# Second block's attention: decay added to masks on GpSimd, division before the turn, values stationary on column halves

## The chip, the cores and the metric

One NeuronCore of a Trainium2 chip runs the kernel. The metric is the device time of one execution in microseconds, median of several; less is better. The engines are TensorE (PE; its weight loads are listed as PEld), VectorE (DVE), ScalarE (ACT), GpSimd (POOL) and SyncE (SP), which only issues DMAs here. Each works through its own queue in program order and waits on semaphores.

## What is computed

Two blocks of two layers each, one sequence of 256 tokens, 1024 features, all in float32. The change lies in the hybrid mixer of the second block. It has four heads of causal attention with rotary positions (A), four heads of forgetting attention (B), a gated branch (C) and a pooling branch (D); the parts that matter, shortened:

```python
def forgetting_attention(q, k, v, log_f):          # 4 heads of 64, 256 tokens
    c = jnp.cumsum(log_f, axis=-1)
    ...
        logits = (jnp.einsum('bhqd,bhkd->bhqk', qc, k) * scale
                  + cq[..., :, None] - c[..., None, :])
        logits = jnp.where(kpos[None, :] <= qpos[:, None], logits, -jnp.inf)
        p = jax.nn.softmax(logits, axis=-1)
        return jnp.einsum('bhqk,bhkd->bhqd', p, v)

def hybrid_mixer(x, w_in, ...):
    z = x @ w_in
    aq, ak, av, bq, bk, bv, bf, cu, cv, dp = jnp.split(z, IN_SPLITS, axis=-1)
    ya = moba_attention(rotary(aq), rotary(ak), av)     # causal softmax attention here
    yb = forgetting_attention(bq, bk, bv, log_sigmoid(bf + b_forget))
    yc = causal_spatial_gating(gelu(cu), gelu(cv), ...)
    yd = multiscale_pool(dp, pool_w, pool_scale)
    return jnp.concatenate([ya, yb, yc, yd], axis=-1) @ w_o
```

The softmax of a row doesn't change when a number is added to all of it, so of the decay only `-c[k]`, one row of 256 numbers for each head, has to be added to the scores.

## The kernel before

All weights stream through in **units** of 128 x 1024 numbers. SyncE loads a unit into `w_raw` (4 buffers), ScalarE rounds it to `w_hi` (`hi_next`), VectorE makes the difference `w_lo` (`lo_next`, line 1114), and TensorE multiplies with both, so that a float32 product is three float32r ones. `w_hi` and `w_lo` have 6 buffers. ScalarE rounds unit `u` when TensorE has finished unit `u-6`, so ScalarE's and VectorE's steps run beside TensorE's units, and weights are ready about five units ahead.

A second-block mixer (`mixer2`, one for each of two layers) has 26 units. Each engine's program is one loop over unit numbers `i`, with the attention's steps written in at fixed numbers. On TensorE, units 4 to 13 give q and k of four head pairs and the pooling input, 14 to 17 the values `v_tok`, 18 to 25 the output projection over the branches in the order C, D, A, B (`K_OUT`). The steps between, ahead of the unit of that number:

- units 8, 10, 12, 14: `scores(pair)`. Two heads of a pair lie on the two halves of the partitions and run together. For the forgetting pairs 2 and 3 a second product adds the decay: `head_sel` (a column of ones and zeros) times `neg_rows`, the rounded rows of `-c`, which VectorE writes in `split_decay`.
- units 10 to 17: `turn_a(h)`, three transposes of head `h`'s probabilities `sm`. It waits on the exp (`e2_ready`).
- unit 19: `values()`: for each head the turned probabilities `aT8` are the weights and 64 columns of `v_tok` move; the result has tokens on partitions.
- unit 21: `turn_o()`: eight transposes of `o_tok` bring the result to features on partitions.

On VectorE, step `i` holds `attn_mask(i-8)` (adds the causal mask to the scores, takes the row maximum and its negative) for steps 8 to 15, then the weight difference, then what else is due: the rotary steps at 7 and 9 (ahead of the weight difference), `sgu_scale` at 11, the window sums of branch D at 14 and 15, `c_rest` at 15, `o_scale` at 19 (division by the row sums and a factor, token by token), `o_rest` at 21. On ScalarE, step `i` holds a weight rounding, then `attn_store(i-10)`, then `attn_exp(i-8)`, which also sums the rows into `den`. GpSimd clears pads and masks one weight at the start of the mixer and has nothing to do after that, but for a parameter load later on.

## Time and profile before

| | us |
|---|---|
| median of 3 runs | 1910.05 (1909.76 to 1910.22) |
| profiled execution: its span, first to last instruction | 1908.1 |
| TensorE busy | 1899.0 |
| VectorE busy | 1312.4 |
| ScalarE busy | 1112.2 |
| GpSimd busy | 8.6 |

The profile gives its own execution's time as the span; the timed runs' median stands 1.95 us above it. The page counts an instruction busy from start to end, and matmuls overlap: a start of one to a start of the next is what an instruction costs the queue. Times in the rows are from the span's start. A float32 product stands in the trace as two matmuls (two passes) and a transpose as one. The form `128*64` behind a matmul is the part of the array used, rows by columns.

### The profile page before, as it was taken

What the parts mean: (1) busy time and instruction counts of PE and PEld (TensorE: products, weight loads), DVE (VectorE), ACT (ScalarE), POOL (GpSimd) and SP (SyncE); (2) the same over time, 40 slices, a digit from 0 to 9 for tenths busy, and PEclk for the clock granted to TensorE, in tenths of its full rate; (3) what the DMA queues carried; (4) which work ended last, traced back from release to release, by engine and by line L of the source; (5) the groups of instructions that cost most, each with busy time, mean ns of one, the idle gap of its engine ahead of it and who ended that gap; (6) DMA issues with size and microseconds to landing.
All of it is one profiled execution on the core that took longest, in us unless ns stands there. A gap on an engine that the chain in (4) does not pass through costs nothing.

```text
span 1908.1 us, 26525 instructions
## 1 busy us (share of the span) xinstructions
PE 1899.0 (100%) x10072; PEld 1610.6 (84%) x10072; DVE 1312.4 (69%) x2238; ACT 1112.2 (58%) x1738; POOL 8.6 (0%) x22
## 2 busy tenths in 40 slices
PE   9999999999999999999999999999999999999998
PEld 7888899888888888888988888888988888988887
DVE  6555887585755575558876767555868888868887
ACT  6444766554644564457764556445747666747664
POOL 0000000000000000000000000000000000000000
PEclk9999999999999999999999999999999999999999
DMA  8555445545655555555455446554535555535552
GB/s 303 190 188 183 161 140 168 166 154 188 206 188 187 177 188 188 187 166 177 133 177 164 159 163 218 199 190 153 177 111 190 193 190 194 179 111 189 192 193 100
DMA packets 92654, 337.74 MB, mean 177 GB/s; under 512 B 10288, under 2 KB 10544, under 8 KB 92400
## 3 DMA queue, kind: packets, MB, share of 16 engines
q1 hardware_dynamic: 91152, 329.49, 52.0%
q0 software_dynamic: 1232, 6.47, 1.0%
q8 instruction: 81, 1.33, 0.3%
q14 instruction: 45, 0.37, 0.1%
q10 hardware_dynamic: 144, 0.09, 0.0%
HBM read 334.96 MB, written 1.05 MB: 176 GB/s over the span
## 4 chain that ended last, share of the span: by engine, by line
PE 98%; DVE 1%; ACT 0%; DMA 0%; issue 0%; DVEq 0%; SPq 0%; ACTq 0%
PE stream L1971 14%; PE stream L1973 14%; PE stream L1972 14%; PE acc L1971 9%; PE acc L1973 9%; PE acc L1972 9%; PE stream L2457 7%; PE stream L2458 4%; PE stream L1965 4%; PE stream L1966 3%; PE stream L1967 3%; PE stream L2063 1%; PE acc L2175 1%; PE stream L1991 1%; PE acc L2224 0%; PE acc L2457 0%
## 5 line engine op out<-in xcount | busy, mean ns | idle before, releaser
L1114 DVE TENSOR_TENSOR w_lo<-w_raw,w_hi 128x1024 fp32r<-128x1024 f32 x623 | 759.0, 1223 | 371.1 <-ACT w_hi L585 369.1
L585 ACT ACTIVATE w_hi<-w_raw 128x1024 fp32r<-128x1024 f32 x623 | 654.7, 1055 | 389.4 <-PE stream L1973 271.7
L1971 PE MATMUL stream<-w_hi,h_both 128*128 128x512 f32 x1024 | 405.0, 396 | 0.0
L1973 PE MATMUL stream<-w_lo,h_both 128*128 128x512 f32 x1024 | 399.0, 390 | 0.0
L1972 PE MATMUL stream<-w_hi,h_both 128*128 128x512 f32 x1024 | 398.8, 389 | 0.0
L1971 PEld LDWEIGHTS stream<-w_hi,h_both 128*128 128x128 f32 x1024 | 192.3, 188 | 41.6 <-DVE h_both L1597 0.8
L1973 PEld LDWEIGHTS stream<-w_lo,h_both 128*128 128x128 f32 x1024 | 192.2, 188 | 40.8
L1972 PEld LDWEIGHTS stream<-w_hi,h_both 128*128 128x128 f32 x1024 | 192.5, 188 | 37.8
L2457 PE MATMUL stream<-h_both,w_hi 128*128 128x512 f32 x608 | 216.1, 398 | 0.0
L1971 PE MATMUL acc<-w_hi,act_hi 128*128 128x512 f32 x528 | 211.1, 400 | 0.3
L1973 PE MATMUL acc<-w_lo,act_hi 128*128 128x512 f32 x528 | 206.3, 391 | 0.0
L1972 PE MATMUL acc<-w_hi,act_lo 128*128 128x512 f32 x528 | 206.2, 390 | 0.0
L2458 PE MATMUL stream<-h_both,w_lo 128*128 128x256 f32 x608 | 170.6, 281 | 0.0
L1965 PE MATMUL stream<-h_both,w_hi 128*128 128x256 f32 x544 | 159.1, 292 | 0.0
L1966 PE MATMUL stream<-h_both,w_hi 128*128 128x256 f32 x544 | 153.7, 283 | 0.0
L1967 PE MATMUL stream<-h_both,w_lo 128*128 128x256 f32 x544 | 153.7, 283 | 0.0
L2457 PEld LDWEIGHTS stream<-h_both,w_hi 128*128 128x128 f32 x608 | 114.2, 188 | 27.6
L1971 PEld LDWEIGHTS acc<-w_hi,act_hi 128*128 128x128 f32 x528 | 99.2, 188 | 21.8 <-DVE w_lo L1114 1.9
L1973 PEld LDWEIGHTS acc<-w_lo,act_hi 128*128 128x128 f32 x528 | 99.1, 188 | 21.7
L2458 PEld LDWEIGHTS stream<-h_both,w_lo 128*128 128x128 f32 x608 | 114.8, 189 | 1.4
L1972 PEld LDWEIGHTS acc<-w_hi,act_lo 128*128 128x128 f32 x528 | 99.3, 188 | 17.9
L1965 PEld LDWEIGHTS stream<-h_both,w_hi 128*128 128x128 f32 x544 | 104.0, 191 | 2.0 <-issue 1.2
(347 smaller groups left out, 2433.7 us busy)
## 6 DMA issues: line engine op xcount, KB each, us to landing
w_raw<-in_w_up SPq DMA_DIRECT2D x264, 512.0 KB, 3.4
w_raw<-in_w_mix SPq DMA_DIRECT2D x228, 512.0 KB, 3.4
w_raw<-in_w_down SPq DMA_DIRECT2D x132, 512.0 KB, 3.4
params<-in_params POOLq DMA_DIRECT2D x4, 859.5 KB, 6.1
x_residual<-in_x SPq DMA_DIRECT2D x4, 256.0 KB, 5.5
constants<-in_params POOLq DMA_DIRECT2D x2, 512.0 KB, 8.7
last_gain_bias<-in_last POOLq DMA_DIRECT2D x1, 1024.0 KB, 5.1
out_x<-y_tok SPq DMA_DIRECT2D x4, 256.0 KB, 2.1
```

Of the source, the lines that this page charges most:

```text
L585: nc.scalar.activation(w_hi[:, u % RING], w_raw[:, u % RAW], ACT.Copy).then_inc(hi_ready, 1)
L1114: nc.vector.tensor_tensor(w_lo[:, u % RING], w_raw[:, u % RAW], w_hi[:, u % RING].bitcast(F32), ALU.subtract).then_inc(split_done, 1)
L1965: nc.tensor.matmul(dst, w_hi[:, s, w], hi, start=first, stop=False)
L1966: nc.tensor.matmul(dst, w_hi[:, s, w], lo, start=False, stop=False)
L1967: return nc.tensor.matmul(dst, w_lo[:, s, w], hi, start=False, stop=last)
L1971: nc.tensor.matmul(dst, hi, w_hi[:, s, w], start=first, stop=False)
L1972: nc.tensor.matmul(dst, lo, w_hi[:, s, w], start=False, stop=False)
L1973: return nc.tensor.matmul(dst, hi, w_lo[:, s, w], start=False, stop=last)
L1991: r = nc.tensor.transpose(turned[q][:, half(j)], y_tok[:, t, (4 * q + j) * P:(4 * q + j + 1) * P], ident)
L2063: r = nc.tensor.transpose(dst, cbuf[:, 2 * (c % 2) + t, half(i)], ident)
L2457: nc.tensor.matmul(dst, w_hi[:, u % RING, w], h_both[:, k], start=(k == 0), stop=False)
L2458: r = nc.tensor.matmul(dst[:, 0:T], w_lo[:, u % RING, w], h_hi[:, k], start=False, stop=(k == KT - 1))
```

## The change

- The decay is no longer multiplied onto the scores. GpSimd stores the four rows of `-c` to DRAM, loads them back to all 128 partitions (`mask_keys`), and adds the causal mask to them; `attn_mask` of heads 4 to 7 uses these instead of `mask_rows`. The rounded rows, the selector and `split_decay` are gone.
- The probabilities are divided by their row sums before they are turned: VectorE takes the reciprocal of a head's two columns (`invert`, at the start of step 9+h), GpSimd multiplies `sm` in place, and `turn_a` waits for GpSimd (`p_divided`) in place of the exp.
- In `values()` the 64 columns of `v_tok` are the weights and the turned probabilities move, 256 and 128 columns; the two heads of a pair write to the two halves of the partitions. The result already has features on partitions. `turn_o`, `o_tok` and `o_scale` are gone; ScalarE and VectorE round the result from PSUM with the factor `BRANCH`, at step 20 instead of 21.

```diff
...
@@ -479,7 +478,7 @@
 
         V_FM, V_C1, V_OUT = 4, 14, 18
         FM_UNITS = 10
-        HEAD_AT, TURN_AT, VALUES_AT, OUT_TURN_AT = 8, 10, 19, 21
+        HEAD_AT, TURN_AT, VALUES_AT, OUT_AT = 8, 10, 19, 20
         K_OUT = (4, 5, 6, 7, 0, 1, 2, 3)
         EVICTIONS = 2 + FM_UNITS + 2
 
...
@@ -1003,10 +1002,10 @@
                                                  scale=pool_sc[:, ct:ct + 1])
                     r.then_inc(cd_hi, 1)
 
-                def o_round(t):
-                    act.wait_ge(o2_turned, l * 2 + t + 1)
-                    nc.scalar.activation(ya_hi[:, 0:4, half(t)], bank[2 * t + 1][:].rearrange("p (k q) -> p k q", k=4),
-                                         ACT.Copy).then_inc(o2_hi, 1)
+                def o_round(g):
+                    act.wait_ge(o2_ready, l * 2 + g + 1)
+                    nc.scalar.activation(ya_hi[:, 2 * g:2 * g + 2].rearrange("p a t -> p (a t)"), bank[2 * g][:],
+                                         ACT.Copy, scale=BRANCH).then_inc(o2_hi, 1)
 
                 def take_gelu(t):
                     if t == 0:
...
@@ -1699,17 +1698,6 @@
                     dve.wait_ge(f_vec, l * 3 + 2)
                     nc.vector.tensor_scalar(neg_c[:], row2_c[:], -1.0 / A_SCALE, None, ALU.mult).then_inc(f_vec, 1)
 
-                def split_decay():
-                    dve.wait_ge(f_vec, l * 3 + 3)
-                    if l == 0:
-                        dve.wait_ge(neg_cleared, 1)
-                    for b in (0, 64):
-                        nc.vector.tensor_copy(neg_rows[b:b + 4], neg_c[:]).then_inc(neg_split, 1)
-                    dve.wait_ge(neg_split, l * 4 + 2)
-                    for b in (32, 96):
-                        nc.vector.tensor_tensor(neg_rows[b:b + 4], neg_c[:], neg_rows[0:4].bitcast(F32),
-                                                ALU.subtract).then_inc(neg_split, 1)
-
                 def groups(ap):
                     return ap.rearrange("p a (g c) -> p a g c", c=64)
 
...
@@ -1777,10 +1765,13 @@
                     dve.wait_ge(s2_ready, l * 8 + h + 1)
                     if h >= 2:
                         dve.wait_ge(a2_turned, l * 8 + h - 1)
+                    if h == 4:
+                        dve.wait_ge(decay_ready, (l + 1) * 2)
+                    mask = mask_rows if h < 4 else mask_keys[:, h - 4]
                     nc.vector.memset(spare[:, 13 + b:14 + b], 0.0)
                     for qt, (lo, hi) in enumerate(((0, P), (P, 3 * P))):
                         r = nc.vector.tensor_tensor_reduce(
-                            out=sm[:, b, lo:hi], in0=side[b][:, lo:hi], in1=mask_rows[:, lo:hi], scale=1.0,
+                            out=sm[:, b, lo:hi], in0=side[b][:, lo:hi], in1=mask[:, lo:hi], scale=1.0,
                             scalar=-3e38, op0=ALU.add, op1=ALU.max,
                             accum_out=mx[:, 2 * b + qt:2 * b + qt + 1])
                     r.then_inc(s2_masked, 1)
...
@@ -1818,30 +1809,20 @@
                                                            op0=ALU.mult, op1=ALU.subtract)
                     r.then_inc(cd_split, 1)
 
-                def o_scale():
-                    dve.wait_ge(e2_ready, l * 8 + 8)
-                    nc.vector.reciprocal(rden[:], den[:]).then_inc(dve_step, 1)
-                    dve.wait_ge(dve_step, stepped())
-                    nc.vector.tensor_scalar(rden[:], rden[:], BRANCH, None, ALU.mult).then_inc(dve_step, 1)
-                    dve.wait_ge(dve_step, stepped())
-                    for t in range(QT):
-                        dve.wait_ge(o2_ready, l * 2 + t + 1)
-                        nc.vector.tensor_tensor(o_tok[:, t].rearrange("p (h d) -> p h d", h=HEADS),
-                                                bank[2 - 2 * t][:].rearrange("p (h d) -> p h d", h=HEADS),
-                                                rden[:, :, t].unsqueeze(2).to_broadcast([P, HEADS, 64]),
-                                                ALU.mult).then_inc(o2_scaled, 1)
-
-                def o_rest(t):
-                    dve.wait_ge(o2_hi, l * 2 + t + 1)
-                    nc.vector.tensor_tensor(ya_lo[:, 0:4, half(t)], bank[2 * t + 1][:].rearrange("p (k q) -> p k q", k=4),
-                                            ya_hi[:, 0:4, half(t)].bitcast(F32), ALU.subtract).then_inc(ab_split, 1)
-
-                if l == 0:
-                    for b in (0, 64):
-                        r = nc.vector.tensor_tensor(head_sel[b:b + 64], ident[b:b + 64, b:b + 4],
-                                                    ident[b:b + 64, b + 32:b + 36], ALU.add)
-                    r.then_inc(sel_ready, 1)
+                def invert(h):
+                    dve.wait_ge(e2_ready, l * 8 + h + 1)
+                    nc.vector.reciprocal(rden[:, h], den[:, h]).then_inc(den_ready, 1)
+
+                def o_rest(g):
+                    dve.wait_ge(o2_hi, l * 2 + g + 1)
+                    nc.vector.scalar_tensor_tensor(out=ya_lo[:, 2 * g:2 * g + 2].rearrange("p a t -> p (a t)"),
+                                                   in0=bank[2 * g][:], scalar=BRANCH,
+                                                   in1=ya_hi[:, 2 * g:2 * g + 2].rearrange("p a t -> p (a t)").bitcast(F32),
+                                                   op0=ALU.mult, op1=ALU.subtract).then_inc(ab_split, 1)
+
                 for i in range(U_MIX2 - LAG + 1):
+                    if HEAD_AT < i <= HEAD_AT + HEADS:
+                        invert(i - HEAD_AT - 1)
                     if HEAD_AT <= i < HEAD_AT + HEADS:
                         attn_mask(i - HEAD_AT)
                     if i == 7:
...
@@ -1919,6 +1896,22 @@
                 w = p2("sgu_w", 0, 4 * P).rearrange("p (g t) -> p g t", g=4)
                 nc.gpsimd.tensor_tensor(w, w, mask_cols.unsqueeze(1).to_broadcast([P, 4, P]),
                                         ALU.mult).then_inc(sgu_w_masked, 1)
+                pool.wait_ge(f_vec, l * 3 + 3)
+                pool.dma_start(decay_dram[l], neg_c[:]).then_inc(decay_out, 16)
+                pool.wait_ge(decay_out, (l + 1) * 16)
+                pool.dma_start(mask_keys[:, :, 0:P], decay_dram[l][:, 0:P].partition_broadcast(P)).then_inc(decay_in, 16)
+                pool.dma_start(mask_keys[:, :, P:], decay_dram[l].partition_broadcast(P)).then_inc(decay_in, 16)
+                pool.wait_ge(decay_in, (l + 1) * 32)
+                for c in (slice(0, P), slice(P, 3 * P)):
+                    nc.gpsimd.tensor_tensor(mask_keys[:, :, c], mask_keys[:, :, c],
+                                            mask_rows[:, c].unsqueeze(1).to_broadcast([P, 4, c.stop - c.start]),
+                                            ALU.add).then_inc(decay_ready, 1)
+                for h in range(HEADS):
+                    b = h % 2
+                    pool.wait_ge(den_ready, l * 8 + h + 1)
+                    for t, c in enumerate((slice(0, P), slice(P, 3 * P))):
+                        r = nc.gpsimd.tensor_scalar(sm[:, b, c], sm[:, b, c], rden[:, h, t:t + 1], None, ALU.mult)
+                    r.then_inc(p_divided, 1)
 
             pool.wait_ge(raw_full[2], 3 * 16)
             pool.dma_start(cst[:, 3 * P:C_LATE], consts[:, 3 * P:C_LATE]).then_inc(consts_in, 16)
...
@@ -2539,36 +2530,24 @@
                     r.then_inc(swapped, 1)
 
                 def scores(pair):
-                    forgets = pair >= 2
                     q, k = 2 * pair, 2 * pair + 1
                     if pair == 0:
                         pe.wait_ge(f_vec, l * 3 + 2)
                     else:
                         pe.wait_ge(s2_masked, l * 8 + 2 * pair)
-                    if forgets:
+                    if pair >= 2:
                         pe.wait_ge(m2_evict, e0 + 2 + k + 1)
-                        pe.wait_ge(neg_split, l * 4 + 4)
-                        pe.wait_ge(sel_ready, 1)
                     else:
                         pe.wait_ge(rot_done, l * 2 + pair + 1)
                     for qs, ks, c in ((slice(P, T), T, slice(P, 3 * P)), (slice(0, P), P, slice(0, P))):
                         for j in range(2):
                             r = slice(64 * j, 64 * j + 64)
-                            i = nc.tensor.matmul(side[j][:, c], qk[r, q, qs], qk[r, k, 0:ks], start=True,
-                                                 stop=not forgets)
-                            if ks == P and not forgets:
+                            i = nc.tensor.matmul(side[j][:, c], qk[r, q, qs], qk[r, k, 0:ks], start=True, stop=True)
+                            if ks == P:
                                 i.then_inc(s2_ready, 1)
-                        if forgets:
-                            for j in range(2):
-                                r = slice(64 * j, 64 * j + 64)
-                                col = 2 * (pair - 2) + j
-                                i = nc.tensor.matmul(side[j][:, c], head_sel[r, col:col + 1].to_broadcast([64, P]),
-                                                     neg_rows[r, 0:ks], start=False, stop=True)
-                                if ks == P:
-                                    i.then_inc(s2_ready, 1)
 
                 def turn_a(h):
-                    pe.wait_ge(e2_ready, l * 8 + h + 1)
+                    pe.wait_ge(p_divided, l * 8 + h + 1)
                     if h > 0:
                         pe.wait_ge(a2_stored, l * 8 + h)
                     for b in range(3):
...
@@ -2579,22 +2558,15 @@
                     pe.wait_ge(m2_evict, e0 + EVICTIONS)
                     pe.wait_ge(a2_stored, l * 8 + HEADS)
                     pe.wait_ge(cd_split, l * 2 + 2)
-                    for h in range(HEADS):
-                        c = slice(64 * h, 64 * h + 64)
-                        r = nc.tensor.matmul(bank[2][:, c], aT8[:, h, 0:P], v_tok[:, 0, c], start=True, stop=True)
-                    r.then_inc(o2_ready, 1)
-                    for h in range(HEADS):
-                        c = slice(64 * h, 64 * h + 64)
-                        nc.tensor.matmul(bank[0][:, c], aT8[:, h, P:T], v_tok[:, 0, c], start=True, stop=False)
-                        r = nc.tensor.matmul(bank[0][:, c], aT8[:, h, T:], v_tok[:, 1, c], start=False, stop=True)
-                    r.then_inc(o2_ready, 1)
-
-                def turn_o():
-                    for t in range(QT):
-                        pe.wait_ge(o2_scaled, l * 2 + t + 1)
-                        for k in range(4):
-                            r = nc.tensor.transpose(bank[2 * t + 1][:, blk(k)], o_tok[:, t, blk(k)], ident)
-                        r.then_inc(o2_turned, 1)
+                    for j in range(HEADS // 2):
+                        at = j % 2 * T
+                        for keys, rows, c in ((0, slice(0, T), slice(at, at + T)), (1, slice(T, 3 * P), slice(at + P, at + T))):
+                            for h in (2 * j, 2 * j + 1):
+                                z = 64 * (h % 2)
+                                r = nc.tensor.matmul(bank[j // 2 * 2][z:z + 64, c], v_tok[:, keys, 64 * h:64 * h + 64],
+                                                     aT8[:, h, rows], start=keys == 0, stop=keys == 1)
+                        if j % 2:
+                            r.then_inc(o2_ready, 1)
 
                 def mixed(u):
                     k = K_OUT[u - u0 - V_OUT]
@@ -2603,7 +2575,7 @@
                 def arrived(u):
                     k = K_OUT[u - u0 - V_OUT]
                     if k < 4:
-                        pe.wait_ge(ab_split, l * 2 + 2)
+                        pe.wait_ge(ab_split, l * 2 + k // 2 + 1)
                     else:
                         pe.wait_ge(cd_split, l * 2 + (k - 4) // 2 + 1)
 
@@ -2635,8 +2607,6 @@
                         pooling()
                     if i == VALUES_AT:
                         values()
-                    if i == OUT_TURN_AT:
-                        turn_o()
                     u = u0 + i
                     unit(u)
                     if i < V_C1:
```

Left out are the declarations: `decay_dram` (a DRAM tensor for each layer) and `mask_decayed` come, `o_tok`, `neg_rows`, `head_sel` and their semaphores go, and `OUT_TURN_AT`, 21, becomes `OUT_AT`, 20.

VectorE's queue at the end of the heads, steps 15 and 16 of a mixer, before (`w_lo` is a weight difference, `pool_sums` and `pooled` the window sums, `ya_lo` the rest of branch C):

```order
L1788 TENSOR_SCALAR neg_max<-row_max 128x2
L1114 TENSOR_TENSOR w_lo<-w_raw,w_hi 128x1024
L1798 SCALAR_TENSOR_TENSOR pool_sums<-constants,pool_in 128x256
L1803 TENSOR_TENSOR pooled<-pool_sums 64x256 x2
L1809 TENSOR_TENSOR pooled<-pooled,constants 128x512
L1811 TENSOR_TENSOR pooled<-pooled,pool_in 128x512
L1755 SCALAR_TENSOR_TENSOR ya_lo<-acc,ya_hi 128x512
L1114 TENSOR_TENSOR w_lo<-w_raw,w_hi 128x1024 x2
```

and in the changed kernel, from the same instruction on, the mask of head 7:

```order
L1779 TENSOR_SCALAR neg_max<-row_max 128x2
L1113 TENSOR_TENSOR w_lo<-w_raw,w_hi 128x1024
L1789 SCALAR_TENSOR_TENSOR pool_sums<-constants,pool_in 128x256
L1794 TENSOR_TENSOR pooled<-pool_sums 64x256 x2
L1800 TENSOR_TENSOR pooled<-pooled,constants 128x512
L1802 TENSOR_TENSOR pooled<-pooled,pool_in 128x512
L1743 SCALAR_TENSOR_TENSOR ya_lo<-acc,ya_hi 128x512
L1814 RECIPROCAL row_scales<-row_sums 128x2
L1113 TENSOR_TENSOR w_lo<-w_raw,w_hi 128x1024 x2
```

The reciprocal of head 7 stands behind all of step 15, ahead of two weight differences.

GpSimd's queue in the first mixer, before (the last row loads the next layer's parameters):

```order
L1941 MEMSET neg_c_rounded 128x256
L1918 MEMSET pool_sums 128x2x16
L1920 ISA
L1920 TENSOR_TENSOR params<-params,constants 128x512
L1929 DMA params<-in_params 128x1719
```

and in the changed kernel (`neg_c_rows` is in DRAM; the last two rows are the division of head 0 and come eight times, once for each head):

```order
L1895 MEMSET pool_sums 128x2x16
L1897 ISA
L1897 TENSOR_TENSOR params<-params,constants 128x512
L1900 DMA neg_c_rows<-row_neg_c 4x256
L1902 DMA mask_decayed<-neg_c_rows 128x4x128
L1903 DMA mask_decayed<-neg_c_rows 128x4x256
L1906 TENSOR_TENSOR mask_decayed<-mask_decayed,constants 128x4x128
L1906 TENSOR_TENSOR mask_decayed<-mask_decayed,constants 128x4x256
L1913 TENSOR_SCALAR scores<-scores,row_scales 128x128
L1913 TENSOR_SCALAR scores<-scores,row_scales 128x256
```

Head 0's division stands behind the store, the two loads and the two sums.

## Rows read from the trace of the kernel before

**Rows 1.** The page: busy time and share by engine; the chain by engine.
```profile
PE 1899.0 (100%) x10072; PEld 1610.6 (84%) x10072; DVE 1312.4 (69%) x2238; ACT 1112.2 (58%) x1738; POOL 8.6 (0%) x22
...
PE 98%; DVE 1%; ACT 0%; DMA 0%; issue 0%; DVEq 0%; SPq 0%; ACTq 0%
```

**Rows 2.** Stretches: length, busy PE, PEld, DVE, ACT, POOL, clock, DMA share, GB/s.
```profile
1343.64:1412.51 68.87, 68.80 (x491) 63.16 (x488) 51.78 (x115) 40.92 (x84) 0.00 (x0) 1.00 0.49 161
1629.97:1698.85 68.88, 68.81 (x491) 63.17 (x488) 49.86 (x113) 39.55 (x83) 0.00 (x0) 1.00 0.46 153
```

**Rows 3.** Timeline, PE: start, length, line, result<-operands; scores and turns.
```profile
1364.00 0.92 PE L2557 MATMUL acc<-qk 64*128 64x256 f32 x8
1364.85 0.55 PE L2575 MATMUL stream<-constants,scores 128*128 128x128 f32 x3
...
1371.39 0.70 PE L2557 MATMUL acc<-qk 64*128 64x256 f32 x4
...
1372.43 0.55 PE L2575 MATMUL stream<-constants,scores 128*128 128x128 f32 x3
```

**Rows 4.** Timeline, PE: values, the next unit, and the turn of the result.
```profile
1398.25 1.89 PE L2584 MATMUL stream<-v_tok,attn_T 128*128 128x64 f32 x16
...
1403.52 0.48 PE L1971 MATMUL acc<-w_hi,ya_hi 128*128 128x512 f32 x1
...
1409.10 1.04 PE L2596 MATMUL stream<-constants,o_tok 128*128 128x128 f32 x8
...
1410.20 0.39 PE L1972 MATMUL acc<-w_hi,ya_lo 128*128 128x512 f32 x1
```

**Rows 5.** Timeline, PE: first block's gate rows; full-width 256-column passes (L2537).
```profile
224.65 1.95 PE L2151 MATMUL stream<-x_residual,params 128*64 128x256 f32 x16
...
226.75 0.28 PE L1966 MATMUL stream<-h_both,w_hi 128*128 128x256 f32 x1
...
1352.38 1.03 PE L2537 MATMUL acc<-qk,constants 128*128 128x256 f32 x4
...
1353.36 0.28 PE L1966 MATMUL stream<-h_both,w_hi 128*128 128x256 f32 x1
```

**Rows 6.** Timeline, DVE: weight differences behind branch C; a reciprocal.
```profile
1390.86 2.40 DVE L1114 TENSOR_TENSOR w_lo<-w_raw,w_hi 128x1024 fp32r<-128x1024 f32 x2
...
1400.73 0.25 DVE L1823 RECIPROCAL row_scales<-row_sums 128x16 f32<-128x16 f32 x1
```

**Rows 7.** Timeline, PE: the turn of head 7.
```profile
1390.68 0.49 PE L2575 MATMUL stream<-constants,scores 128*128 128x128 f32 x3
```

**Rows 8.** Timeline, POOL: its work at the start of the first mixer.
```profile
1330.32 0.31 POOL L1941 MEMSET neg_c_rounded<- 128x256 f32 x1 [118.26 <-PE acc L1973]
...
1330.74 1.08 POOL L1920 TENSOR_TENSOR params<-params,constants 128x512 f32<-128x512 f32 x1
```

**Rows 9.** Timeline, DVE, beside GpSimd's sum and after it.
```profile
1330.75 0.35 DVE L1152 SCALAR_TENSOR_TENSOR x_residual<-stream,gains,x_residual 128x128 f32<-128x128 f32 x1
1331.01 0.90 DVE L1118 TENSOR_SCALAR h_both<-x_residual,gains 128x128 fp32r<-128x128 f32 x1
...
1332.35 0.28 DVE L1118 TENSOR_SCALAR h_both<-x_residual,gains 128x128 fp32r<-128x128 f32 x1
```

**Rows 10.** Timeline, DVE: the decay rows; two steps of pair 1's rotation.
```profile
1351.85 0.28 DVE L1700 TENSOR_SCALAR row_neg_c<-row_c 4x256 f32<-4x256 f32 x1
...
1362.44 0.69 DVE L1771 TENSOR_TENSOR qk<-qk,constants 128x512 f32<-128x512 f32 x1
1363.16 0.69 DVE L1773 TENSOR_TENSOR qk<-qk,rotated 128x512 f32<-128x512 f32 x1
```

**Rows 11.** DMA issues: what, queue, count, size, us from issue to landing.
```profile
constants<-in_params POOLq DMA_DIRECT2D x2, 512.0 KB, 8.7
last_gain_bias<-in_last POOLq DMA_DIRECT2D x1, 1024.0 KB, 5.1
out_x<-y_tok SPq DMA_DIRECT2D x4, 256.0 KB, 2.1
```

25 lines of the change are left out of this document (9 added, 16 removed).

## The prediction

> **What bounds the kernel now.** I read the page first: TensorE is busy for the whole span and holds 98% of the chain that ended last [rows 1]. Then the busy times of the two stretches that the change touches, unit 4 to unit 22 of each second-block mixer: TensorE 68.80 of 68.87 us and 68.81 of 68.88 us, at a granted clock of 1.00, which is the 2.4 GHz level [rows 2]. So there is no wait on TensorE to win. What the change takes off TensorE's queue comes off the time, and every wait that it adds there is paid in full. VectorE (52 us) and ScalarE (41 us) have room on average, but not everywhere, and GpSimd does nothing in these stretches. Last I read the timeline around the places that change. Both mixers show the same rows, 286 us apart on TensorE, so each term is worked out for the first and taken twice.
>
> **What leaves TensorE.** (a) The decay products. Scores of pair 1, which has none, go from 1364.00 to the next instruction at 1364.85, 0.85 us; pair 2, with them, from 1371.39 to 1372.43, 1.04 us [rows 3]. Two pairs: 0.38 us.
> (b) The values. They now run from 1398.25 to 1403.52, 5.27 us: 24 products of 64 columns, each split into two passes, so that 0.11 us a pass is mostly the change of weights [rows 4]. The new form exists already in the first block: the gate rows, 8 products with 64 stationary columns written to partition halves, 256 moving columns, 16 passes. They take from 224.65 to 226.63 (0.12 before the matmul at 226.75), 1.98 us, where a full-width pass of 256 columns takes 0.215 (four from 1352.38 to 1353.24) and 16 of them would take 3.44 [rows 5]. So two halves do run side by side, and 1.98 holds the way in and out. The new values have as many such passes, 1.98, and 16 of 128 columns; eight 128-column passes in a row take 0.87 [rows 4], which two at a time prices 16 at. Together 2.85, so 2.42 us less.
> (c) The turn of the result: from 1409.10 to 1409.97 (0.23 before 1410.20), 0.87 us [rows 4].
> A mixer saves 0.38 + 2.42 + 0.87 = 3.67 us on TensorE, two save 7.3. VectorE also loses the rounding of the decay rows, the scaling of the result and its reciprocal, and gains eight small reciprocals; weights and rounding run units ahead, so of these only the ones inside the head chain below count.
>
> **What is added: a divide between exp and turn.** Before, a head's chain was mask (VectorE), exp (ScalarE), turn (TensorE). Now it is mask, exp, reciprocal (VectorE), two multiplications (GpSimd), turn. The turn of head h waits on TensorE, ahead of unit 10+h, and all units queue behind it. I went through the heads by asking when VectorE gets to the reciprocal, since it stands in program order at the start of step 9+h. Heads 1 to 6 have most of two units between exp and turn, more than the new steps need. Head 7 has nothing left: its reciprocal stands behind the whole of the window sums and the rest of branch c. VectorE ends those at 1390.86, where it now goes on to two weight differences [rows 6], while TensorE starts turn 7 at 1390.68 [rows 7]. In the changed kernel VectorE has one more reciprocal (head 6) ahead of that, 0.2, and the one of head 7, 0.2 (a reciprocal of 128x16 took 0.25 [rows 6]): 1391.25. GpSimd's two multiplications have 384 columns. By the clearing of 256 columns in 0.31 they take 0.46, by the sum of two operands over 512 in 1.08 they take 0.81 [rows 8]; one operand and a result lie between, I take 0.65. That gives 1391.9 against 1390.68 - 0.38 = 1390.3 for TensorE: **a wait of 1.6 us** if nothing else is in the way.
> Something is. While GpSimd's sum ran (1330.74 to 1331.82), a VectorE multiplication that reads and writes SBUF alone took 0.90 instead of 0.28 and ended with it; a VectorE instruction with one operand from PSUM took its usual 0.35 beside the same sum [rows 8, 9]. So the two engines hold each other up on SBUF. Right behind the reciprocal of head 7 VectorE goes into two weight differences, all in SBUF, 2.40 us [rows 6]. They are ready and start at once; GpSimd needs a semaphore first. If they hold up GpSimd as its sum held up VectorE, it gets in behind the second, or one multiplication behind each: 1391.25 + 2.4 + 0.65 = 1394.3, **a wait of 4.0 us**. The ends are 1.6 and 4.0; I take 4.0, since the row nearest to a difference of two SBUF tiles is the multiplication in SBUF that was held, not the one fed from PSUM.
> The Trainium skill, SBUF — State Buffer, section "Who interferes with whom", goes further than the row: a VectorE instruction with two SBUF inputs and a GpSimd instruction that reads SBUF exclude each other for a whole instruction, and the one that started first goes on. By it the wait is the 4.0 of the sum above; if it held for VectorE's two-port modes alone, which is all that the row shows, it would be the 1.6.
>
> **What is added: decay rows through DRAM.** GpSimd's queue holds, in this order, the store of the rows, a wait for it, two broadcast loads, a wait for them, two sums, then the divide of head 0. So head 0, which needs no decay at all, and TensorE's turn 0 behind it, wait for the whole transfer. The rows are ready at 1352.13 [rows 10]. The store: a small store took 2.1 (256 KB) [rows 11], 1354.2. The loads, 0.79 MB in 1024 pieces: issue 0.6, and 5.1 to landing as for 1 MB, 8.7 at worst [rows 11]; I take 5.1 as the nearest in size: 1359.9. The sums: 512 and 1024 columns at 1.08 per 512, 3.2 us: 1363.1. The divide 0.65: 1363.8, against turn 0 at 1364.85 [rows 3]. **Wait 0**; with 8.7 it would be 2.5.
> The Trainium skill, DMA: Bandwidth & Descriptors, "Anatomy of one DMA — SWDGE (gpsimd) path", prices a GpSimd DMA at 2.0 us plus its bytes over 436 GB/s, 3.8 us for the loads; the divide would then end at 1362.5, and the wait stays 0.
> The sums have a second price. They fall on 1359.9 to 1363.1, where VectorE rotates pair 1 (1362.44, 1363.16, both in SBUF [rows 10]) and TensorE's scores of pair 1 start at 1364.00, 0.15 us behind the rotation's end. The reciprocal of head 0 stands ahead of it as well, 0.2. So TensorE waits between 0.2 (no hindrance) and 2.4 (a rotation step that finds the longer sum just begun, 2.2 more). I take the middle, **1.3 us**, because the sums cover the first of the two steps for half of their length.
> The mask of head 4 needs the sums only behind turn 2, at 1372.43 [rows 3], and between the values and the reader of the newly rounded result stand three units, of which 19 and 20 alone take 1403.52 to 1409.10 [rows 4], more than two evictions on ScalarE and VectorE need: both at no price, the first at one for one if the sums came after 1372.43.
>
> **The sum.** Per mixer -3.67 + 4.0 + 1.3 + 0 = +1.6, twice +3.3 us. Made against the span of 1908.1 us that is 1911.4, and the time stands 1.95 us above the span, as the median of the runs does now: 1913.4 us. Some 0.2% (3.8 us) is what a measurement of this kernel can tell from no change, so the forecast lies at the edge of it.
>
> **Rivals.**
> 1. No mutual hindrance with weight differences and rotations: waits of 1.6 and 0.2, -3.67 + 1.8 = -1.9 per mixer, 1906.3 us, faster. For it: the VectorE instruction with PSUM input was not slowed. Against: the one in SBUF was, threefold.
> 2. The loads land late (1024 small pieces where the rows have 128 large ones, beside weight traffic). It decides from a landing about 1 us after 1359.9. At 8.7 the divide ends at 1367.4; the rotation is then free of the sums (0.2), turn 0 waits 2.3 to 3.5, per mixer +2.9 to +4.0: 1916 to 1918 us, slower.
> 3. TensorE's clock falls during the 4 us wait. No row shows a price, since TensorE never stands still here. If the lower level, 1.2 GHz, lasted as long as the wait, 2 us per mixer are lost: 1917 us.
> 4. The halves don't run side by side: values 16 x 0.215 + 16 x 0.11 = 5.2, nothing saved in (b), 1918 us. [rows 5] speak against it.
>
> **How the numbers follow.** Forecast 0.50 (its own range 1910.5 to 1917: the rotation term alone gives 2 us either way), rival 1 0.27, rival 2 0.13, rival 3 0.07, rival 4 0.03. Of the forecast's share about half lies over 1913.9 (slower), of rival 1's a little over half under 1906.2 (faster), and rivals 2 to 4 are nearly all slower: slower 0.25 + 0.21 = 0.46, faster 0.16, same 0.38. The range takes in rival 1 with a shorter GpSimd price and rivals 2 to 4 at their middle: 1905.5 to 1919.
>
> **What would show it.** TensorE's idle time ahead of turn 7: 4 us (forecast) or 1.6 (rival 1), its releaser GpSimd's second multiplication. GpSimd's multiplications of head 7 starting only after a weight difference ends, or weight differences longer than 1.2 us beside them. Idle time ahead of scores 1 released by a rotation that is longer than 0.69 us [rows 10]. Values 2.85 us. The first sum starting at about 1360; after 1361, rival 2. What would make it wrong most easily is the size of the hindrance, which rests on one row.

## The result and the profile after

| | us |
|---|---|
| changed kernel, median of 4 runs | 1926.55 (1924.31 to 1928.18) |
| the kernel before beside it, median of 4 | 1909.91 (1909.76 to 1910.22) |
| ratio, with its 95% interval | 1.0085 [1.0073, 1.0098] |
| profiled execution of the changed kernel: span | 1922.5 (its time 1924.31) |

The change makes the kernel slower by 0.85%, about 17 us. The forecast was 1913.4, the range ended at 1919.0. The profiled execution is the shortest of the four; its span grew by 14.4 us, from 1908.1 to 1922.5, and the rest of this section says where they lie. The other three, 1.0 to 3.9 us longer, have no trace. The page, busy time and chain, against [rows 1]:

```profile
PE 1899.1 (99%) x10008; PEld 1605.9 (84%) x10008; DVE 1312.3 (68%) x2236; ACT 1113.1 (58%) x1738; POOL 55.1 (3%) x63
...
PE 92%; DVE 4%; POOL 1%; DMA 1%; ACT 1%; issue 1%; POOLq 0%; DVEq 0%; ACTq 0%
```

TensorE has 64 matmuls fewer and is busy for as long as before: either nothing was saved, or what remains runs slower. It has lost 6% of the chain to others. The saving is real. The values in the second mixer, timeline of TensorE:

```profile
1702.42 2.82 PE L2566 MATMUL stream<-attn_T,v_tok 128*64 128x256 f32 x32
1705.17 0.50 PE L1962 MATMUL acc<-w_hi,ya_hi 128*128 128x512 f32 x1
```

From 1702.42 to 1705.17 are 2.75 us where [rows 4] had 5.27. With the turn of the result (0.8) and the decay products (0.38) a mixer saves 3.7 us, as predicted; two save 7.4. The waits are in the same timeline; the last bracket is TensorE's idle time ahead of the row and who ended it. First mixer, then the second:

```profile
1365.49 0.92 PE L2545 MATMUL acc<-qk 64*128 64x256 f32 x8 [1.10 <-DVE qk L1761]
1370.08 0.90 PE L2554 MATMUL stream<-constants,scores 128*128 128x128 f32 x3 [3.66 <-POOL scores L1913]
1395.83 0.55 PE L2554 MATMUL stream<-constants,scores 128*128 128x128 f32 x3 [0.46 <-POOL scores L1913]
1402.39 0.55 PE L2554 MATMUL stream<-constants,scores 128*128 128x128 f32 x3 [3.26 <-POOL scores L1913]
...
1662.35 1.58 PE L2545 MATMUL acc<-qk 64*128 64x256 f32 x8 [1.98 <-DVE qk L1761]
1664.10 0.90 PE L2554 MATMUL stream<-constants,scores 128*128 128x128 f32 x3 [0.17 <-POOL scores L1913]
1688.14 0.55 PE L2554 MATMUL stream<-constants,scores 128*128 128x128 f32 x3 [0.46 <-POOL scores L1913]
1694.70 0.55 PE L2554 MATMUL stream<-constants,scores 128*128 128x128 f32 x3 [3.26 <-POOL scores L1913]
```

In order: scores of pair 1, then turns 0, 6 and 7. Before there was no such bracket here. They add up to 14.35 us. Rows 1370.08 and 1664.10 show something else: three transposes take 0.90 us where they took 0.55. The stretches behind the waits tell why (length, busy time of PE, PEld, DVE, ACT, POOL, then the granted clock, DMA share and GB/s):

```profile
1370.08:1374.90 4.82, 4.82 (x23) 4.82 (x24) 2.08 (x8) 1.48 (x5) 2.93 (x4) 0.50 0.37 136
1374.90:1376.00 1.10, 1.10 (x8) 1.10 (x8) 0.00 (x0) 0.00 (x0) 0.00 (x0) 0.62 0.73 291
...
1402.39:1403.40 1.01, 1.01 (x6) 0.90 (x7) 0.00 (x0) 0.42 (x1) 0.00 (x0) 0.83 0.74 199
1403.40:1405.60 2.20, 2.20 (x7) 1.72 (x6) 0.27 (x1) 0.91 (x3) 0.00 (x0) 0.50 0.46 182
1405.60:1408.00 2.40, 2.40 (x10) 1.88 (x9) 0.60 (x2) 0.60 (x1) 0.00 (x0) 0.82 0.00 0
1662.30:1663.00 0.70, 0.65 (x4) 0.66 (x6) 0.70 (x1) 0.00 (x0) 0.70 (x1) 0.61 0.00 0
1663.00:1664.90 1.90, 1.73 (x12) 1.41 (x9) 0.41 (x2) 0.00 (x0) 1.90 (x3) 0.50 0.26 95
1664.90:1667.00 2.10, 2.10 (x16) 2.10 (x16) 1.82 (x7) 1.42 (x5) 0.63 (x1) 0.77 0.43 164
```

A clock of 0.50 is the 1.2 GHz level; [rows 2] had 1.00 all through. Busy time times the missing share of the clock gives what is lost: 2.83 us behind turn 0 and 1.70 behind turn 7 of the first mixer, 1.60 behind scores of pair 1 of the second, 6.1 in all. Behind turn 7 of the second mixer the clock stayed at 1.00. So -7.4 + 14.35 + 6.1 = +13.1 of the 14.4. Of the other 1.3, about 0.5 had arisen by 306 us, in the first block, which is the same in both kernels; what makes the rest is not shown.

Two timelines hold the causes. GpSimd in the first mixer (store, two loads, two sums, divisions of heads 0 and 1 together, then heads 5 and 7):

```profile
1352.35 0.58 POOL L1900 DMA_DIRECT2D neg_c_rows<-row_neg_c  x1 [20.11 <-DVE row_neg_c L1699]
1357.01 0.80 POOL L1902 DMA_DIRECT2D mask_decayed<-neg_c_rows  x1 [4.08 <-DMA neg_c_rows<-row_neg_c]
1357.81 0.77 POOL L1903 DMA_DIRECT2D mask_decayed<-neg_c_rows  x1
1363.52 4.04 POOL L1906 TENSOR_TENSOR mask_decayed<-mask_decayed,constants 128x512 f32<-128x512 f32 x2 [4.94 <-DMA mask_decayed<-neg_c_rows]
1367.54 3.97 POOL L1913 TENSOR_SCALAR scores<-scores,row_scales 128x128 f32<-128x128 f32 x4
...
1387.37 1.51 POOL L1913 TENSOR_SCALAR scores<-scores,row_scales 128x128 f32<-128x128 f32 x2 [2.48 <-DVE row_scales L1814]
...
1398.98 3.36 POOL L1913 TENSOR_SCALAR scores<-scores,row_scales 128x128 f32<-128x128 f32 x2 [3.20 <-DVE row_scales L1814]
```

and VectorE (last rotation step of pair 1, a weight difference; then the reciprocal of head 7 and the difference behind it):

```profile
1363.69 1.66 DVE L1761 TENSOR_TENSOR qk<-qk,rotated 128x512 f32<-128x512 f32 x1
1365.27 3.37 DVE L1113 TENSOR_TENSOR w_lo<-w_raw,w_hi 128x1024 fp32r<-128x1024 f32 x1
...
1398.73 0.15 DVE L1814 RECIPROCAL row_scales<-row_sums 128x2 f32<-128x2 f32 x1
1398.80 1.20 DVE L1113 TENSOR_TENSOR w_lo<-w_raw,w_hi 128x1024 fp32r<-128x1024 f32 x1
```

A head's two multiplications take 1.51 us when nothing disturbs them, and 3.36 beside two weight differences. In the other direction a rotation step takes 1.66 instead of 0.69 [rows 10], and a difference 3.37 instead of 1.20, beside GpSimd's sums.

### The profile page after: what moved, and what is told of

It is laid out like the page before. It is cut to its first block, busy times and chain, and to the rows that moved or that the text cites. A ratio compares the mean times of both kernels' runs of the same rounds, so it can differ in the third digit from the quotient of the medians.

```text
span 1922.5 us, 26430 instructions
## 1 busy us (share of the span) xinstructions
PE 1899.1 (99%) x10008; PEld 1605.9 (84%) x10008; DVE 1312.3 (68%) x2236; ACT 1113.1 (58%) x1738; POOL 55.1 (3%) x63
## 4 chain that ended last, share of the span: by engine, by line
PE 92%; DVE 4%; POOL 1%; DMA 1%; ACT 1%; issue 1%; POOLq 0%; DVEq 0%; ACTq 0%
PE stream L1962 13%; PE stream L1963 13%; PE stream L1964 13%; PE acc L1962 9%; PE acc L1964 8%; PE acc L1963 8%; PE stream L2448 7%; PE stream L2449 4%; PE stream L1956 3%; PE stream L1957 3%; PE stream L1958 3%; PE stream L2054 1%; POOL scores L1913 1%; DVE w_lo L1113 1%; PE acc L2166 1%
```

## The experiments

The theory after the result: (i) GpSimd's division is slower than I priced it, and it and VectorE hold each other up; (ii) GpSimd's fixed order makes head 0 pay for the decay rows; (iii) each long wait costs more than itself, since TensorE's clock falls behind it. The rivals: the low clock has another cause; GpSimd or VectorE is simply too full. Each ratio is against runs of the kernel before taken beside it, with medians of 1910.47, 1910.21 or 1910.07 us. Where two effects meet in one kernel, its profiled execution is used for the account and the median for the verdict.

**A wait alone.** The kernel before, with TensorE made to stand still ahead of turn 7:

```diff
+                pool.wait_ge(unit_done, mix2_at(l) + TURN_AT + 7)
+                pool.dma_start(pause_dram[l], neg_c[:]).then_inc(pause, 16)
...
                     pe.wait_ge(e2_ready, l * 8 + h + 1)
+                    if h == 7:
+                        pe.wait_ge(pause, (l + 1) * 16)
```

> The kernel before, with one standstill of TensorE added in each second-block mixer: ahead of the turn of head 7 it also waits for a 4 KB store that GpSimd issues when unit 16 ends (a store of this size took 3.6 and 4.6 us in the changed kernel). Nothing else is altered. Theory (the clock falls behind a wait and this has a price of its own): the time rises by the two idle times, some 8 us, and by 1.4 to 2.6 us more for each of them behind which the granted clock falls to the 1.2 GHz level: 1919 to 1923 us, and the rows behind the wait show a clock of 0.50 for 2.8 to 5.3 us. Rival (a wait costs its own length and no more; the low clock in the changed kernel has another cause): 1918 us, the clock stays at 1.00.

Measured 1916.72 us, ratio 1.0031 [1.0019, 1.0044]. The idle times, and the clock in the stretch behind each:

```profile
1392.85 0.52 PE L2582 MATMUL stream<-constants,scores 128*128 128x128 f32 x3 [2.30 <-issue]
...
1681.63 0.52 PE L2582 MATMUL stream<-constants,scores 128*128 128x128 f32 x3 [2.25 <-issue]
```
```profile
1392.85:1398.00 5.15, 5.15 (x29) 4.46 (x30) 0.99 (x3) 2.91 (x6) 0.00 (x0) 1.00 0.60 197
1681.63:1686.60 4.97, 4.97 (x17) 4.02 (x18) 1.03 (x3) 1.88 (x4) 0.00 (x0) 0.66 0.96 349
```

The store was quicker than expected, so the waits are 4.55 us in all and the time, up by 6.2, lies below both numbers expected. The clock fell behind one of two waits of equal length, and there 4.97 x 0.34 = 1.7 us went: theory (iii), at the price that it named.

**A longer wait.** The store is issued twice, the second behind the first (`for j in range(2)`, TensorE waits for both).

> As the kernel before with one standstill ahead of turn 7, but GpSimd issues the 4 KB store twice, the second when the first has landed, so that TensorE stands still for some 4.6 us instead of 2.3 in each mixer. With one store the time rose by 6.0 us for 4.55 us of idle time, with the low clock behind one of the two. Theory (a longer standstill makes the fall certain, the price of a fall stays at 1.5 to 2.6 us): the clock falls in both mixers, the time rises by 9.2 us of idle time and 3 to 5 us: 1922.5 to 1924.5 us. Rival (whether it falls does not depend on the length): one fall or none, 1919.5 to 1921 us.

Measured 1927.68 us, 1.0091 [1.0076, 1.0107], above the 1924.5 expected. The waits were 6.39 and 6.37, not 4.6; the clock fell behind both:

```profile
1397.22:1402.40 5.18, 5.18 (x17) 4.29 (x18) 0.88 (x2) 1.93 (x4) 0.00 (x0) 0.65 0.00 0
1691.86:1698.00 6.14, 6.14 (x17) 4.96 (x18) 0.88 (x2) 1.92 (x4) 0.57 (x1) 0.52 0.47 171
```

17.6 us less 12.8 of waiting leave 4.8, or 2.4 a fall (by the two rows 1.8 and 2.9).

**The decay rows by products again.** The store, loads and sums of the change go out, the old `split_decay` and the products in `scores` come back; the division stays on GpSimd.

```diff
-                pool.dma_start(decay_dram[l], neg_c[:]).then_inc(decay_out, 16)
...
-                    mask = mask_rows if h < 4 else mask_keys[:, h - 4]
...
+                                i = nc.tensor.matmul(side[j][:, c], head_sel[r, col:col + 1].to_broadcast([64, P]),
+                                                     neg_rows[r, 0:ks], start=False, stop=True)
```

> The changed kernel with the decay rows added as before, by products on TensorE into the scores, so without the transfer through DRAM and without GpSimd's sums; division stays on GpSimd. Theory (the late loads and the sums make the waits at scores 1 and turn 0, 4.76 us in the first mixer and 2.15 in the second, with the low clock behind them): both waits are under 0.5 us, turns 6 and 7 keep 0.46 and 3.26, the decay products cost 0.38 a mixer: 1909.9 - 7.4 + 0.8 + 2 x (3.7 + 0.3) and 0 to 2.8 for the clock behind turn 7 = 1911.3 to 1914.1 us. Rival (the division, not the decay path, makes turn 0 late): the wait at turn 0 stays at 2 us or more, over 1918 us.

Measured 1917.93 us, 1.0040 [1.0027, 1.0052]: 8.6 less than the change, but 4 more than I expected. The waits at scores of pair 1 went altogether, so the sums made them, and turn 0 does not wait in either mixer, so the decay rows made that wait too. In their place 1.05 and 1.01 us stand ahead of turn 1. TensorE, GpSimd (divisions of heads 1 and 2 together) and VectorE (the rounding of the decay rows that came back, ahead of head 1's reciprocal), first mixer:

```profile
1369.87 0.55 PE L2573 MATMUL stream<-constants,scores 128*128 128x128 f32 x3 [1.05 <-POOL scores L1918]
```
```profile
1367.23 4.07 POOL L1918 TENSOR_SCALAR scores<-scores,row_scales 128x128 f32<-128x128 f32 x4 [3.92 <-DVE row_scales L1822]
```
```profile
1366.07 0.86 DVE L1709 TENSOR_TENSOR neg_c_rounded<-row_neg_c,neg_c_rounded 4x256 fp32r<-4x256 f32 x2
```

VectorE comes to that reciprocal 1.5 us later for it, at 1366.97, and a weight difference then meets head 1's second multiplication: 2.01 us instead of 0.92. Turns 6 and 7 kept 0.43 to 0.46 and 3.26, and this time the clock fell behind turn 7 in both mixers. The account: 2 x 3.3 us saved, 9.5 of waits and 3.4 of clock make +6.3 of the 8.2 by which the profiled span grew over that of the kernel before; 1.9 stay open. The same sum leaves 0.1 for the pause and, below, 0.3 for the early reciprocal, 1.0 for VectorE held back and 1.1 for the sums behind head 2.

**The same with the wait filled.** Ahead of turn 7 in that kernel TensorE gets three products that nobody reads:

```diff
                 def turn_a(h):
-                    pe.wait_ge(p_divided, l * 8 + h + 1)
                     if h > 0:
                         pe.wait_ge(a2_stored, l * 8 + h)
+                    for _ in range({(0, 7): 3, (1, 7): 3}.get((l, h), 0)):
+                        nc.tensor.matmul(bank[3][:], ident, cst[:, 0:512], start=True, stop=True)
+                    pe.wait_ge(p_divided, l * 8 + h + 1)
```

> The kernel with the decay rows by products and the division on GpSimd (1917.9 us, 3.26 us of idle TensorE ahead of turn 7 in both mixers, low clock behind both), with three products of 512 columns that nobody reads put on TensorE ahead of each turn 7, inside the wait. By the 0.86 us that such a product should take they fill 2.6 of the 3.26 us. Theory (the clock falls because TensorE stands idle): turn 7 starts when it did, the clock behind it stays at 1.00, and 1.5 to 1.8 us per mixer come back: 1914.3 to 1915 us. Rival (the low clock behind turn 7 comes from something else than the idle time): no less than 1917.5 us, clock 0.75 to 0.8 in the 8 us behind turn 7 as before.

Measured 1915.24 us, 1.0026 [1.0016, 1.0036], 2.7 less by doing more, 0.2 above the range that I gave. The stretch behind turn 7 without the filling, both mixers:

```profile
1396.56:1402.50 5.94, 5.94 (x23) 4.84 (x24) 0.88 (x2) 2.08 (x5) 0.00 (x0) 0.71 0.31 106
1686.90:1692.80 5.90, 5.90 (x22) 4.78 (x23) 0.88 (x2) 2.02 (x5) 0.50 (x1) 0.71 0.74 274
```

and with it, the filling and the turn first:

```profile
1392.51 2.73 PE L2572 MATMUL stream<-constants 128*128 128x512 f32 x6
1395.92 0.55 PE L2575 MATMUL stream<-constants,scores 128*128 128x128 f32 x3 [0.68 <-POOL scores L1918]
```
```profile
1395.92:1401.90 5.98, 5.97 (x32) 5.12 (x33) 1.04 (x3) 3.47 (x6) 0.00 (x0) 1.00 0.32 104
1684.86:1690.80 5.94, 5.94 (x32) 5.12 (x33) 1.04 (x3) 3.47 (x6) 0.50 (x1) 1.00 0.79 277
```

Turn 7 waits for the same GpSimd division and starts about as late (2.73 of filling and 0.68 of standing still for 3.26). The clock does not fall, and 32 matmuls fit where 23 did. That shows it for these two waits: standing still is what costs the clock, and the clock is what costs beyond the wait.

**VectorE held back at head 7.** The changed kernel with one wait:

```diff
+                    if i == HEAD_AT + HEADS:
+                        dve.wait_ge(p_divided, (l + 1) * 8)
                     lo_next()
```

> The changed kernel, with VectorE's two weight differences behind the reciprocal of head 7 held back until GpSimd has divided head 7. Theory (the two engines exclude each other on SBUF; undisturbed the two multiplications take 1.51 us as they do for heads 2 and 5): GpSimd's 3.36 us become 1.5, TensorE's idle time ahead of turn 7 goes from 3.26 to 1.4 us in both mixers, and the 1.4 us of low clock behind turn 7 of the first mixer go as well: 3.7 to 5 us less than the changed kernel, 1921.5 to 1923 us. Rival (GpSimd is slow at head 7 for a reason of its own, such as its place in the program or the semaphore): the wait stays at 3.26 and the time at 1926.5 us.

Measured 1921.03 us, 1.0055 [1.0042, 1.0069]. GpSimd's division of head 7, VectorE's differences behind it, TensorE's wait:

```profile
1399.25 1.51 POOL L1915 TENSOR_SCALAR scores<-scores,row_scales 128x128 f32<-128x128 f32 x2 [3.20 <-DVE row_scales L1814]
```
```profile
1400.79 2.36 DVE L1113 TENSOR_TENSOR w_lo<-w_raw,w_hi 128x1024 fp32r<-128x1024 f32 x2 [1.64 <-POOL scores L1915]
```
```profile
1400.81 0.55 PE L2556 MATMUL stream<-constants,scores 128*128 128x128 f32 x3 [1.41 <-POOL scores L1915]
```

1.51 instead of 3.36, and 1.41 instead of 3.26, to the number expected, by making VectorE wait. The mutual hindrance is shown. So is its limit: 1.4 us stay, and these are GpSimd's own length. No clock fell behind turn 7. The median is 5.5 less than the change where 3.7 to 5 were expected, though in the profiled execution two waits that the edit does not touch were longer: scores of pair 1 and turn 0 stood 4.04 and 1.43 us in the first mixer, for 1.10 and 3.66.

**The reciprocal of head 7 early.** The changed kernel, VectorE's step 15:

```diff
-                    if HEAD_AT < i <= HEAD_AT + HEADS:
+                    if HEAD_AT < i < HEAD_AT + HEADS:
                         invert(i - HEAD_AT - 1)
...
                     if i == 15:
+                        invert(7)
                         window_sums(1)
```

> The changed kernel with one reciprocal moved on VectorE: that of head 7 ahead of the second half of the window sums and of branch c's rounding, and not behind them. In the changed kernel exp of head 7 had ended at 1394.93 and VectorE came to the reciprocal at 1398.73. Theory (3.8 us of the lateness of turn 7 is the place of the reciprocal in VectorE's order): even at 3.4 us for the division it ends before TensorE arrives, the 3.26 us ahead of turn 7 go in both mixers, the low clock behind it as well, and at most 0.5 us come back where the pooling waits for window sums that are held up: 1918 to 1920 us against 1926.5. Rival (GpSimd's division beside the window sums costs as much as it cost behind them, by holding up the sums that the pooling waits for): the wait moves from turn 7 to the pooling, 1923 us or more.

Measured 1917.55 us, 1.0037 [1.0025, 1.0050], 9 us less for one line moved. That is just under what the theory gave: turn 7 does not wait in either mixer, and neither does the pooling. Turn 0 of the first mixer stands at 3.65 as before, with the low clock behind it.

**The sums behind head 2.** Only GpSimd's order is changed: the wait for the loads and the two sums go behind the division of head 2.

```diff
-                pool.wait_ge(decay_in, (l + 1) * 32)
-                for c in (slice(0, P), slice(P, 3 * P)):
...
                 for h in range(HEADS):
...
                     r.then_inc(p_divided, 1)
+                    if h == 2:
+                        pool.wait_ge(decay_in, (l + 1) * 32)
+                        for c in (slice(0, P), slice(P, 3 * P)):
...
```

> The changed kernel with one thing moved on GpSimd: the wait for the decay loads and the two sums stand behind the division of head 2 and not ahead of that of head 0; the store, its wait and the loads stay in front. Theory (head 0, which needs no decay, was held by GpSimd's order; the sums met pair 1's rotation): the wait ahead of turn 0 is 1.1 us in both mixers, as with the decay rows by products, that at scores of pair 1 under 0.3, the low clock behind turn 0 of the first mixer goes, turn 7 keeps its 3.26: 1926.3 - 3.7 - 1.3 - 2.6 = 1916 to 1919 us. Rival (the sums harm wherever they stand, since 4 us of GpSimd on SBUF hold up masks or divisions of heads 3 and 4): waits of 1.5 us or more at turns 3 to 5, 1921 us or more.

Measured 1924.90 us, 1.0075 [1.0063, 1.0088]: the rival, by time and by mechanism. Turn 0 does not wait any more and scores of pair 1 wait 0.48 at most, so head 0 was indeed held by the decay rows. (The 1.1 us that I expected ahead of turn 0 was a misreading: with the decay rows by products it stands ahead of turn 1.) But now turn 3 waits. GpSimd (the sums, then the divisions of heads 3 and 4), VectorE beside the sums (a weight difference, a step of branch C), TensorE:

```profile
1370.09 4.65 POOL L1913 TENSOR_TENSOR mask_decayed<-mask_decayed,constants 128x512 f32<-128x512 f32 x2
1376.92 4.02 POOL L1908 TENSOR_SCALAR scores<-scores,row_scales 128x128 f32<-128x128 f32 x4 [2.18 <-DVE row_scales L1814]
```
```profile
1370.29 2.20 DVE L1113 TENSOR_TENSOR w_lo<-w_raw,w_hi 128x1024 fp32r<-128x1024 f32 x1
1372.41 2.88 DVE L1723 TENSOR_TENSOR sgu_normed<-sgu_normed,sgu_rstd 128x512 f32<-128x512 f32 x1
```
```profile
1379.52 0.55 PE L2555 MATMUL stream<-constants,scores 128*128 128x128 f32 x3 [3.24 <-POOL scores L1908]
```

It is not GpSimd's order that holds head 3: GpSimd is done with the sums at 1374.7 and stands for 2.18 us until VectorE has head 3's reciprocal. VectorE is late, because the sums stretched two of its steps from 1.22 to 2.20 and from 0.68 to 2.88. The wait has moved from turn 0 to turn 3, and the clock fell behind three of the four waits of 3.2 us or more. Neither of the two places tried is free for 4 us of sums in one piece.

**The division on VectorE.** GpSimd's loop over the heads goes; decay rows and sums stay.

```diff
                     nc.vector.reciprocal(rden[:, h], den[:, h]).then_inc(den_ready, 1)
+                    dve.wait_ge(den_ready, l * 8 + h + 1)
+                    for t, c in enumerate((slice(0, P), slice(P, 3 * P))):
+                        r = nc.vector.tensor_scalar(sm[:, h % 2, c], sm[:, h % 2, c], rden[:, h, t:t + 1], None, ALU.mult)
+                    r.then_inc(p_divided, 1)
```

> The changed kernel with the division of the exponentials on VectorE, straight behind each reciprocal, and not on GpSimd; decay rows and mask sums stay on GpSimd. Theory (GpSimd's multiplications and their place behind the decay rows are what makes turns 0 and 7 late; VectorE has room for 0.5 us a head): no wait at turn 0, under 0.8 us at turn 7, the wait at scores of pair 1 stays at 1 to 2 us because the mask sums still meet the rotation: 1909.9 - 7.4 + 2 x (0.5 + 1.5) = 1906.5 us, between 1904.5 and 1909, clock 1.00 behind the turns. Rival (VectorE becomes the bound of the head chain: 4 us more work per mixer on it): waits at masks and turns of the middle heads, 1911 us or more.

Measured 1912.15 us, 1.0011 [1.0002, 1.0020], with an unusual spread, 1908.58 to 1917.05 over 11 runs; the median is the rival's number, the fastest run the theory's. In that run, the profiled one, turn 0 does not wait, scores of pair 1 wait 0.90 and 1.68, turn 7 1.39 where I had under 0.8 (the reciprocal ends 0.75 us after TensorE stands there, and the division adds its 0.55), all at a full clock. The rival's mechanism, waits at the middle heads, shows only as 0.42 at turn 1. VectorE takes 0.55 us for a division, but not beside GpSimd's sums (VectorE, then GpSimd):

```profile
1365.75 3.54 DVE L1817 TENSOR_SCALAR scores<-scores,row_scales 128x128 f32<-128x128 f32 x2
```
```profile
1365.19 3.95 POOL L1910 TENSOR_TENSOR mask_decayed<-mask_decayed,constants 128x512 f32<-128x512 f32 x2 [6.29 <-DMA mask_decayed<-neg_c_rows]
```

The spread follows the mean granted clock of the run:

| mean clock | times, us |
|---|---|
| 1.000 | 1908.58, 1910.24, 1910.49 |
| 0.999 | 1909.23, 1911.23 |
| 0.998 | 1912.15, 1912.30, 1913.68 |
| 0.997 | 1915.56, 1916.62 |
| 0.996 | 1917.05 |

About 2 us for each 0.001, which is what 0.001 of a span of 1910 us comes to. That fits one code that meets a fall in some runs and not in others; only the fastest has a trace, so it is not shown, and which waits the falls follow stays open.

**Only what shortens TensorE's queue.** Division on VectorE, that of head 7 ahead of the window sums, decay rows by products; nothing on GpSimd.

> Only the part of the change that shortens TensorE's queue is kept: values on column halves and no turn of the result; the division is on VectorE (0.55 us a head), the one of head 7 ahead of the window sums, and the decay rows come by products as in the kernel before. Nothing is on GpSimd. Theory (all of the loss came from waits and the low clock behind them; the saving on TensorE is real): values 2.75 instead of 5.27 us, 0.81 us for the turn, no wait over 0.3 us in either mixer: 1910.4 - 6.7 = 1903.7 us, between 1903 and 1905.5. Rival (some of the saving is given back behind the values, where the rounding of the result now has one step less ahead of its reader): 1906 us or more, with idle time of TensorE ahead of units 20 to 23.

Measured 1906.24 us (1905.85 to 1906.78), 0.9980 [0.9971, 0.9989]: faster than both kernels, than the one before by 4.0 us where 6.7 were expected. The rival named the right number for a wrong reason: nothing waits behind the values. What is missing is 0.7 us at scores of pair 1 and 0.46 at the pooling, per mixer, where 0.7 us of reciprocal and division now stand ahead of the rotation and of the window sums on VectorE.

**The same with the decay rows through DRAM**, the sums cut into one per head and held until pair 1 is rotated:

```diff
+                pool.wait_ge(rot_done, l * 2 + 2)
+                for j in range(4):
+                    nc.gpsimd.tensor_tensor(mask_keys[:, j], mask_keys[:, j], mask_rows[:],
+                                            ALU.add).then_inc(decay_ready, 1)
```

> As the kernel with the division on VectorE and the reciprocal of head 7 early, but the decay rows come through DRAM as in the change; GpSimd's sums are cut into one per head and wait until pair 1 is rotated. Theory (the sums did harm only where they met work on which TensorE waits): scores of pair 1 wait for nothing, the sums (about 1.2 us each) end ahead of the mask of head 4, and TensorE saves 3.7 us a mixer: 1910.4 - 7.4 = 1903.0 us, up to 1905 with a short wait at turn 1. Rival (the sums hold up VectorE wherever they stand, since the divisions of heads 1 and 2 fall on them): turns 1 or 2 wait 1 us or more, 1906 us or more, and slower than the kernel with products.

Measured 1905.49 us (1905.05 to 1905.74), 0.9975 [0.9965, 0.9985], the best together with the next one, though not the 1903 that I expected. The waits of its first mixer, and GpSimd's four sums:

```profile
1364.52 0.92 PE L2544 MATMUL acc<-qk 64*128 64x256 f32 x8 [0.79 <-DVE qk L1761]
1391.78 1.13 PE L2518 MATMUL stream<-pooled,params 128*128 128x256 f32 x4 [0.45 <-DVE pooled L1802]
```
```profile
1364.53 5.88 POOL L1912 TENSOR_TENSOR mask_decayed<-mask_decayed,constants 128x384 f32<-128x384 f32 x4 [6.60 <-DVE qk L1761]
```

The decay rows through DRAM are worth their 0.38 us a mixer on TensorE (0.75 us for both in the two medians) once no turn depends on GpSimd, even though the sums now take 5.88 us.

**Two moves more on VectorE**: the division of head 0 behind pair 1's rotation, window sums and division of head 7 ahead of step 15's weight difference.

> The kernel with the division on VectorE and the sums cut and held until pair 1 is rotated (1905.5 us), which still stood 0.75 us ahead of scores of pair 1 and 0.46 us ahead of the pooling in each mixer, with two moves on VectorE: the reciprocal and division of head 0 go behind pair 1's rotation, and in step 15 the window sums and the division of head 7 go ahead of that step's weight difference. Theory (these two waits are the 0.75 us of division ahead of the rotation and ahead of the window sums): both go, 2.4 us less: 1903.1 us, 1902.5 to 1904. Rival (turn 0 takes the wait over, since its division now ends 0.7 us later, or turn 7 does): 1904.5 to 1905.5 us.

Measured 1905.46 us (1904.12 to 1905.65), 0.9975 [0.9964, 0.9985]: no gain. In the profiled execution the old waits are gone or 0.23, but turn 0 of the second mixer waits 1.24 and scores of pair 2 in the first 0.34. The rival: part of the wait has only moved. The sums start when the rotation ends, which is now when VectorE divides head 0: in the second mixer that division takes 2.14 us and not 0.55, to 1649.09, and turn 0 starts at 1649.15.

## Why the prediction failed, step by step

| term, both mixers | forecast | measured |
|---|---|---|
| saved on TensorE | -7.3 | -7.4 |
| wait at turn 7 | 8.0 | 6.5 |
| wait at scores of pair 1 | 2.6 | 3.1 |
| wait at turn 0 | 0 | 3.8 |
| wait at turn 6 | 0 | 0.9 |
| clock | 0 | 6.1 |
| the rest, not accounted for | 0 | 1.3 |

- **What leaves TensorE** was right: values 2.75 for an estimate of 2.85. Rival 4 is out.
- **The head chain at turn 7** was right in place and mechanism, as the kernels with VectorE held back and with the early reciprocal show. Two sizes were off and partly cancelled. VectorE came to the reciprocal just before TensorE stood at turn 7 (its end 1398.88, TensorE idle from 1399.13) and not 0.95 us after it. The hold itself was 1.85 us, not 2.40: the two multiplications took 1.50 and 1.88 beside the differences, and the trace shows the first as started beside a difference and not behind it, which was one of the signs that I had named. And undisturbed they cost 1.51 us, not 0.65, beyond my upper end of 0.81. **This is the first step that failed.** I took the price from the columns alone and put one-operand work between clearing and adding. The rows of the changed kernel give 0.605 for 128 columns and 0.92 for 256 (together the 1.51): about 0.29 for each instruction and 2.46 ns a column, no less per column than the two-operand sums (in the second mixer 1.30 and 2.40 us for 512 and 1024 columns, 2.15 ns each). Two instructions pay the 0.29 twice. That heads 1 to 6 have room to spare fails for head 6 by 0.46, and there by the hindrance: its second multiplication took 1.97 beside a weight difference, and with the 0.93 of an undisturbed one it would have been in time. Head 0 is in time when no decay rows stand ahead of it (no wait at turn 0 with the rows by products or the sums behind head 2).
- **The wait at scores of pair 1** was right as a mechanism (it goes without the sums). Its size was luck: the sums came 3.6 us later than forecast, and rival 2 held that the rotation would then be free of them; they met its last step (1.66) in the first mixer and its second (2.37) in the second.
- **The decay rows at turn 0**: my 0 was the second step that failed. Rival 2's wait is what happened, but mostly by the store and GpSimd's own work, not by the landing of the loads that it names. I had the store at 2.1 us by the 256 KB store of SyncE's queue; GpSimd's 4 KB store let the loads start after 4.66 us (1352.35 to 1357.01) and in the second mixer after 3.6. The second load landed 5.7 after its issue (5.1 taken). The sums took 4.04 (3.2 taken), the division of head 0 2.46 (0.65 taken; a weight difference ran beside it). That is 2.8, 0.8 (the loads are two issues of 0.8, where I counted one of 0.6), 0.8 and 1.8 us more, and the division ends 6.2 us behind my 1363.8. A margin of 1.1 us, which is what I had left, was less than two of the chain's four terms were off by alone.
- The Trainium skill, DMA: Bandwidth & Descriptors, section "Anatomy of one DMA — SWDGE (gpsimd) path", has 2.0 us plus bytes over 436 GB/s; the trace of the changed kernel disagrees for both transfers, 3.6 and 4.7 for the store against 2.0, and 5.7 against the 3.8 estimated from the page for the loads; the same store as the pause landed 1.6 us after its issue, nearer the page. The Trainium skill, SBUF — State Buffer, section "Who interferes with whom", has a two-input VectorE instruction and a GpSimd instruction that reads SBUF contend, with the one that came first holding on. The trace agrees at head 7 and at the rotation; the one-input division that took 3.54 instead of 0.55 agrees with the same section's line that such instructions can enter modes in which they use both ports.
- **The clock** was the third and costliest step that failed. I had it as rival 3 with 0.07 and a price of 2 us per mixer. It was there, at 6.1 us in the profiled execution, and the filled wait shows, for turn 7, that it follows from the wait and is no case beside it. I had written that no row shows its price, and then put it at nothing in the forecast.
- **How the cases were combined** made the range too narrow. Forecast, rival 2 and rival 3 stood as alternatives, each on its own, with the far end set by the middle of each alone. They all came at once: by my own prices the forecast's 1913.4 with rival 2's 2.6 to 4.6 and rival 3's 3.6 us on top would have been 1920 to 1922. The terms of the forecast made the rivals likelier: of the waits of 2 to 4 us counted below, 13 of 16 had the low clock behind them, and the forecast itself held one of 4.0 in each mixer.

## What to carry to other kernels

On a kernel whose TensorE never waits, price a new wait at its length plus what the clock gives up behind it, here 1.6 to 2.9 us for each fall; where the wait can't be removed, work without a reader in the gap can be cheaper than standing still (2.7 us for two gaps here). A step moved to an idle engine is only free if it isn't on a chain with a waiting reader: look first at that engine's queue order, then at its undisturbed length, then at whom it shares SBUF with. Rivals that follow from the forecast's own waits add to it; the far end of the range is their sum.

## What the runs showed that was not expected

- The clock's fall is not a plain function of the wait. Taking waits that follow each other closely as one, of the 16 whose longest part was 1.98 to 4.04 us, in the profiled executions of the changed kernel and of the experiments with one pause, the decay rows by products, VectorE held back, the early reciprocal and the sums behind head 2, 13 had a low clock behind them; 2.30 us in one mixer, 3.26 and 3.24 in others did not, while 2.25 did. No single wait of up to 1.7 us in these mixers of a profiled execution had one.
- GpSimd's and VectorE's hindrance goes both ways and can cost several times the instruction's own length: a weight difference of 1.20 us took 3.37, a division of 0.55 took 3.54, and one of 1.51 took 3.36. VectorE lost nothing at head 7 (1.20), where it had begun first.
- A 4 KB store from GpSimd held TensorE for 2.3 us as the pause ahead of turn 7, a second one issued behind it for 4.1 more, and one took 4.7 and 3.6 us in the changed kernel some 40 us earlier in the two mixers. The DMA engines were busy for 0.80 and 0.62 of the time during those two, and for 0.29 and 0.26 around the single pauses. The order fits, but no run separates that traffic from other causes.
